# Seven-product up units of a decoder trunk: operands of VectorE moved from SBUF into PSUM banks

## The reference

```python
h2 = _modulate(_rmsnorm(x, norm_mlp_g[l]), shift2, scale2)
u = jnp.square(jax.nn.relu(h2 @ w_up[l]))        # 1024 -> 4096
x = x + gate2[:, None, :] * (u @ w_down[l])      # 4096 -> 1024
```

## Time and profile before

| | |
|---|---|
| median of three runs | 2293.23 us (2293.02 to 2293.89) |
| the profiled execution | 2292.97 us, span 2291.2 us |
| PE busy | 2259.9 us (99%) |
| DVE busy | 1295.4 us (57%) |
| ACT busy | 959.8 us (42%) |
| POOL busy | 1296.1 us (57%) |
| granted TensorE clock | 0.999 of full speed |

### The profile page before, as it was taken

How to read it: one execution, slowest core, us unless ns; L and a number is a source line. 1 busy time by engine, 2 the same in 40 slices (tenths; PEclk the granted TensorE clock), 3 DMA queues, 4 the chain that set the end, 5 groups by cost and what they waited for, 6 DMA issues and landing times.

```text
span 2291.2 us, 30815 instructions
## 1 busy us (share of the span) xinstructions
PE 2259.9 (99%) x12424; PEld 1922.8 (84%) x12424; DVE 1295.4 (57%) x1695; ACT 959.8 (42%) x1267; POOL 1296.1 (57%) x1538
## 2 busy tenths in 40 slices
PE   7999999999999999999999999999999999999999
PEld 5888888888878888898888888888888789898898
DVE  5876667546653347464576757441666534474563
ACT  4332233256675343343333323233666834343342
POOL 4454554544455458787755455454444444786883
PEclk9999999999999999999999999999999999999999
DMA  9444444422222223323334444222222222323322
GB/s 306 132 157 160 152 134 147 136 67 74 74 93 74 93 92 93 111 93 93 120 124 154 155 147 140 72 92 94 81 70 71 74 92 88 97 93 92 111 92 74
DMA packets 242094, 252.67 MB, mean 110 GB/s; under 512 B 3984, under 2 KB 237600, under 8 KB 241952
## 3 DMA queue, kind: packets, MB, share of 16 engines
q1 hardware_dynamic: 240272, 247.00, 33.4%
q10 hardware_dynamic: 1680, 3.70, 0.5%
HBM read 248.59 MB, written 2.10 MB: 109 GB/s over the span
## 4 chain that ended last, share of the span: by engine, by line
PE 89%; POOL 8%; DVE 1%; ACT 1%; DMA 0%; issue 0%; SPq 0%; DVEq 0%; ACTq 0%
PE proj L1178 54%; PE proj L1201 5%; PE proj L1235 4%; PE att L1218 4%; PE proj L1218 4%; POOL w_lo L486 4%; PE att L1501 3%; PE att L1391 2%; POOL w_lo L491 2%; POOL wx_lo L496 2%; PE att L1441 2%; PE att L1266 2%; PE proj L1266 2%; PE att L1451 1%; PE att L1429 1%; PE att L1373 1%
## 5 line engine op out<-in xcount | busy, mean ns | idle before, releaser
L516 POOL TENSOR_TENSOR w_lo<-w_raw,w_hi 128x256 fp32r<-128x256 f32 x1280 | 1038.1, 845 | 904.6 <-ACT w_hi L562 766.8
L562 ACT ACTIVATE w_hi<-w_raw 128x1024 fp32r<-128x1024 f32 (+1 forms) x300 | 303.8, 1020 | 318.3 <-PE proj L1178 189.2
L1178 PE MATMUL proj<-h_hi,w_hi 128*128 128x512 f32 x1024 | 405.5, 396 | 0.0
L1178 PE MATMUL proj<-h_hi,w_lo 128*128 128x512 f32 x1024 | 399.3, 390 | 0.0
L1178 PE MATMUL proj<-h_lo,w_hi 128*128 128x512 f32 x1024 | 398.8, 389 | 0.0
L1178 PE MATMUL proj<-y_hi,w_hi 128*128 128x512 f32 x784 | 305.2, 389 | 0.0
L1178 PE MATMUL proj<-y_lo,w_hi 128*128 128x512 f32 x784 | 305.1, 389 | 0.0
L1178 PE MATMUL proj<-y_hi,w_lo 128*128 128x512 f32 x784 | 305.0, 389 | 0.0
L1178 PEld LDWEIGHTS proj<-h_hi,w_lo 128*128 128x128 f32 x1024 | 192.1, 188 | 41.2
L1178 PEld LDWEIGHTS proj<-h_hi,w_hi 128*128 128x128 f32 x1024 | 192.4, 188 | 40.4 <-issue 1.6
L1178 PEld LDWEIGHTS proj<-h_lo,w_hi 128*128 128x128 f32 x1024 | 192.5, 188 | 37.6
(11 more groups left out here) (335 smaller groups left out, 4832.6 us busy)
## 6 DMA issues: line engine op xcount, KB each, us to landing
w_raw<-in_w_in SPq DMA_DIRECT2D x88, 1024.0 KB, 5.1
slab<-in_w_ada SPq DMA_DIRECT2D x42, 1024.0 KB, 6.3
w_raw<-in_w_up SPq DMA_DIRECT2D x32, 1024.0 KB, 5.6
w_raw<-in_w_down SPq DMA_DIRECT2D x32, 1024.0 KB, 5.1
w_raw<-in_w_ret_out SPq DMA_DIRECT2D x16, 1024.0 KB, 5.2
w_raw<-in_w_sb_out SPq DMA_DIRECT2D x8, 1024.0 KB, 5.1
w_raw<-in_w_mix_out SPq DMA_DIRECT2D x8, 1024.0 KB, 5.1
ya<-in_x SPq DMA_DIRECT2D x1, 2048.0 KB, 8.1
```

What stands on the lines that cost most here:

```text
L516: ins = pool.tensor_tensor(w_lo[:, slot, k:k + 2, :], w_raw[:, s, k:k + 2, P * j:P * (j + 1)], w_hi[:, slot, k:k + 2, :], ALU.subtract)
L562: ins = act.activation(w_hi[:, 2 * s + j, ks, :], w_raw[:, s, ks, P * j:P * (j + 1)], ACT.Copy)
L1178: last = pe.matmul(proj[:, j, :], w[:, slot, k, :], a[:, k, :], start=k == 0 and n == 0, stop=k == KT - 1 and n == 2)
```

## The change

Four buffers move from SBUF to PSUM, and two steps are written another way.

- `sums_24`, the second pair of weight sums, goes from `ya` to two whole banks: 4 and 5 of `att` for the first unit of a quarter, the two banks of `proj` for the others. `sums_31` stays in SBUF.
- The first output tile is joined in one bank, `FIRST_TILE` (bank 2): product 2 is accumulated in its left half, `joined_11` is added there in place, and `joined_12` is written to its right half. The second is joined in the chain's own bank, `joined_22` in its right half beside product 4 in its left.
- The squares `u_bank(k)` go to banks 4 and 5. ACT now takes the positive part (`Relu`, 128x512) of a joined tile to SBUF, and DVE multiplies that by the joined tile in PSUM; before, DVE squared a tile of SBUF by itself in one instruction. ACT's copy of the chain after product 4 (128x256) goes.
- The banks for products 5 and 3 and for product 2 have one copy each now in place of two, and PE's waits follow: product 5 waits for the join of the unit just before, and product 2 for its square.

The diff, cut to what the prediction speaks of:

```diff
-        sums_24 = ya[:, 6:8, :].rearrange("p a n -> p (a n)").rearrange("p (a i n) -> p a i n", a=2, i=PAIRS)
-        fifth = ada_rows
+        fifth = relu_t[:, 1, 0:HALF]
...
-        def second_bank(q):
-            return att[:, 2 + q % 2, 0:HALF]
-        def fifth_bank(q):
-            return att[:, 4 + q % 2, 0:HALF]
+        FIRST_TILE, FIFTH = att[:, 2, :], att[:, 3, 0:HALF]
+        def u_bank(k):
+            return att[:, 4 + k % 2, :]
+        def sums_24(m):
+            return (att[:, 4:6, :] if m == 0 else proj[:, :, :]).rearrange("p a (i n) -> p a i n", i=PAIRS)
...
-                def take_chain(q):
+                def relu_second(q):
                     act.wait_ge(made[4], q + 1)
-                    act.activation(relu_t[:, 1, 0:HALF], chain_bank(q), ACT.Copy).then_inc(chain_copied, 1)
+                    act.wait_ge(joined_22, q + 1)
+                    act.activation(u_t[:, 1, :], att[:, q % 2, :], ACT.Relu, scale=-1.0).then_inc(u_relued, 1)
                 def up_seven(pair, f, m):
...
                     ahead(0)
+                    if m > 0:
+                        high_u(f, 2 * m - 2)
                     act.wait_ge(made[1], q + 1)
...
                     ahead(2)
+                    if m > 0:
+                        relu_second(q - 1)
                     ahead(3)
-                    if m > 0:
-                        take_chain(q - 1)
                     ahead(4)
...
                     if m > 0:
                         high_u(f, 2 * m - 1)
-                    high_u(f, 2 * m)
+                    act.wait_ge(joined_12, q + 1)
+                    act.wait_ge(joined_11, q + 1)
+                    act.activation(u_t[:, 0, :], FIRST_TILE, ACT.Relu).then_inc(u_relued, 1)
                     if m == 3:
+                        high_u(f, 2 * m)
...
-                    if q >= 2:
-                        pe.wait_ge(joined_12, q - 1)
-                    half_product(5, wx, in_extra(s, 0), t_block(T1), fifth_bank(q), True, False)
+                    if q > 0:
+                        pe.wait_ge(joined_12, q)
+                    half_product(5, wx, in_extra(s, 0), t_block(T1), FIFTH, True, False)
...
-                    if q >= 2:
-                        pe.wait_ge(joined_11, q - 1)
-                    half_product(2, wide, in_slot(2 * s, 1), h_block(1, 0), second_bank(q), True, True)
+                    if m > 0:
+                        pe.wait_ge(u_ready, KT * (4 * layer + f) + 2 * m - 1)
+                    half_product(2, wide, in_slot(2 * s, 1), h_block(1, 0), FIRST_TILE[:, 0:HALF], True, True)
...
-                def square_u(j, bound):
-                    dve.scalar_tensor_tensor(u_t[:, j, :], relu_t[:, j, :], 0.0, relu_t[:, j, :], bound,
+                def square_first(q):
+                    dve.wait_ge(u_relued, 2 * q + 1)
+                    dve.tensor_tensor(u_bank(0), u_t[:, 0, :], FIRST_TILE, ALU.mult).then_inc(u_ready, 1)
+                def square_second(q):
+                    dve.wait_ge(u_relued, 2 * q + 2)
+                    dve.scalar_tensor_tensor(u_bank(1), u_t[:, 1, :], -1.0, att[:, q % 2, :], ALU.mult,
                                              ALU.mult).then_inc(u_ready, 1)
...
                     if m > 0:
+                        square_first(q - 1)
                         join_22(q - 1)
-                        low_u(f, 2 * m - 2)
                     if m < 3:
                         sum_weights(pair, f, m + 1)
+                    if m > 0:
+                        low_u(f, 2 * m - 2)
+                        square_second(q - 1)
+                    if m < 3:
                         low_sums(f, m + 1)
...
                     if m == 3:
+                        square_first(q)
                         join_22(q)
                         low_u(f, 2 * m)
                         square_second(q)
```

More of the change, by code:

```diff
@@ L588, in seven_split @@
                     act.wait_ge(sums_made, 3 * q + 3)
-                    ins = act.activation(wx_hi[:, s, 1:3, :, :], sums_24, ACT.Copy)
+                    ins = act.activation(wx_hi[:, s, 1:3, :, :], sums_24(m), ACT.Copy)
                 else:
@@ L1533, in up_seven @@
                     pe.wait_ge(seven_lo, 3 * q + 1)
-                    if q >= 2:
-                        pe.wait_ge(chain_copied, q - 1)
+                    if m >= 2:
+                        pe.wait_ge(u_ready, KT * (4 * layer + f) + 2 * m - 2)
                     half_product(1, wide, in_slot(2 * s, 0), h_block(0, 0), chain_bank(q), True, False)
@@ L2128, in sum_weights @@
                     dve.wait_ge(sums_made, 3 * q + 1)
-                    dve.scalar_tensor_tensor(sums_24[:, 0, :, :], block[:, A11, :, :], -1.0, sums_31[:, 1, :, :],
+                    dve.scalar_tensor_tensor(sums_24(m)[:, 0, :, :], block[:, A11, :, :], -1.0, sums_31[:, 1, :, :],
                                              ALU.mult, ALU.subtract).then_inc(sums_made, 1)
                     dve.wait_ge(sums_made, 3 * q + 2)
-                    dve.tensor_tensor(sums_24[:, 1, :, :], block[:, A12, :, :], sums_24[:, 0, :, :],
+                    dve.tensor_tensor(sums_24(m)[:, 1, :, :], block[:, A12, :, :], sums_24(m)[:, 0, :, :],
                                       ALU.subtract).then_inc(sums_made, 1)
@@ L2138, in low_sums @@
                     dve.wait_ge(seven_hi, 5 * q + 4)
-                    dve.tensor_tensor(wx_lo[:, s, 1:3, :, :], sums_24, wx_hi[:, s, 1:3, :, :],
+                    dve.tensor_tensor(wx_lo[:, s, 1:3, :, :], sums_24(m), wx_hi[:, s, 1:3, :, :],
                                       ALU.subtract).then_inc(sums_lo, 1)
@@ L2155, in join_22 @@
                     dve.wait_ge(fifth_copied, q + 1)
[L2156 to L2162, removed]
+                    dve.tensor_tensor(att[:, q % 2, HALF:SEQ], fifth, chain_bank(q), ALU.add).then_inc(joined_22, 1)
                 def up_seven(pair, f, m):
@@ L2182, in up_seven @@
                     dve.wait_ge(first_copied, q + 1)
-                    dve.tensor_tensor(relu_t[:, 0, 0:HALF], relu_t[:, 0, 0:HALF], second_bank(q),
+                    dve.tensor_tensor(FIRST_TILE[:, 0:HALF], relu_t[:, 0, 0:HALF], FIRST_TILE[:, 0:HALF],
                                       ALU.add).then_inc(joined_11, 1)
-                    dve.wait_ge(joined_12, q + 1)
-                    dve.wait_ge(joined_11, q + 1)
-                    square_u(0, ALU.max)
+                    dve.wait_ge(made[3], q + 1)
+                    dve.wait_ge(sixth_copied, q + 1)
+                    dve.tensor_tensor(FIRST_TILE[:, HALF:SEQ], relu_t[:, 0, HALF:SEQ], FIFTH,
+                                      ALU.add).then_inc(joined_12, 1)
                     if m == 3:
+                        square_first(q)
                         join_22(q)
```

18 lines of the change are left out of this document (10 added, 8 removed).

## The result

The changed kernel takes 2278.32 us (median of four runs, 2278.23 to 2278.57) against 2293.20 before (2293.02 to 2293.89): a ratio of 0.9935 with a 95% interval of 0.9918 to 0.9952, 14.9 us less. The forecast was 2277.2 us with a range of 2275.5 to 2281.5, and a chance of 0.92 for faster.

A forecast was written before the change was run, and what follows sets the result against it. PE was taken to bound the kernel, held up by POOL's late subtractions in six seven-product quarters. 2292.97 less 16.1, all else at 0, gave 2276.9 us, and 2277.2 with 0.26 for the median; range 2275.5 to 2281.5.

The forecast's parts named there:

- The bound: Six seven-product quarters: PE waits for POOL's late weight subtractions, 2.68 us a quarter, 16.1 us in all to gain.
- The cause: Up units: DVE instructions reading both inputs from SBUF lengthen POOL's subtractions from 0.74 to 1.19 or 1.72 us.
- POOL's need: POOL's ten subtractions of a unit: falls from up to 11.7 to 8.4 us, against PE's 10.1.
- DVE's and ACT's durations: Moved instructions: squares 0.69 us, joins 0.41, Relu 0.60; upper bounds 0.75 and 0.47 for squares and joins.
- The longer way of a tile: Product 2 to product 4 through joins, Relu and square: 2.47 us, hidden inside a quarter, barely in time at its end.
- The slack of 0.13: Quarter's end: join 22 done at 939.15, PE wants product 4 at 939.31; 0.13 us left after a semaphore's 0.03.
- the step of 0.065: DVE's higher fixed cost from PSUM by the Trainium skill: 0.065 us an instruction, one such step lost at the tight hand-over.
- rival A: Down unit: product 4 late at the hand-over, costing 0.2 to 0.7 us a quarter; 2278.4 to 2281.4 us, chance 0.15.
- The shares: Up units: the moved inputs were priced together, POOL's need 11.7 to 8.4 us, for one gain of 16.1 us.
- The sum: Whole kernel: 2292.97 less 16.1 gives 2276.9 us, 2277.2 with the median's 0.26; all other terms at 0.
- B: Up units: POOL stays blocked by DVE's length, output or the two remaining instructions; 2285 to 2293 us, chance 0.07.
- C: Way from product 2 to product 4 bounds a unit if its instructions take near double; 2307 us at double, chance 0.04.

The follow-up runs named there:

- e1: Changed kernel, but the six DVE instructions of a unit whose first input moved to PSUM read x_T in SBUF instead, outputs unmoved: 2295.85 us, ratio 1.0011.
- e4: Kernel before, with squares and splits of u in units 0 to 2 reading one input from a PSUM stand-in: 2277.26 us, ratio 0.9932.
- e5: Changed kernel with one more DVE square ahead of join 22 at the end of each of six quarters: 2281.67 us, ratio 0.9949.
- e2: Kernel before, with only the second pair of weight sums in PSUM, for units 1 to 3 of a quarter: 2277.46 us, ratio 0.9932.
- e8: Changed kernel with 16 waits on a long-passed semaphore added to VectorE's list: 2277.45 us.
- e9: Changed kernel with sums_24 back in SBUF and both splits of u reading x_T in SBUF: 2284.23 us, ratio 0.9961.
- e7: e2 with 108 waits on a long-passed semaphore added to ScalarE's list, 18 in each of six down stretches: 2277.32 us.

## Why the prediction was right

**The bound** (PE loses about 16 us by POOL's lateness, and that is all there is to gain): right. The starts of matmuls moved by 15.5 us, 2.58 a quarter in place of 2.68. Half of the 0.1 is the slow second start that is new at product 4 (0.04 to 0.06); the rest is rounding of the starts that I read.

**The cause** (two inputs from SBUF): right, and shown by e1 in one direction and by e4 in the other, each with the order left alone.

**POOL's need** of 8.4 us a unit: 8.35 measured in the unit shown, 8.3 in the mean. I had priced two blocks at 0.98 + 0.45 = 1.43, and they are 0.87 + 0.45 (subtractions of 1.61 and 1.19 against 0.74). The 11.7 of before was an upper bound and measures 11.1.

**DVE's and ACT's durations**: squares 0.697 against my 0.69, joins 0.422 to 0.429 against 0.41, `Relu` 0.60 against 0.60: right. The higher fixed cost of a PSUM source, which the Trainium skill gives in "VectorE: DVE Perf Modes", section on the errata of SBUF sources, isn't seen here: 0.690 for the split of u from PSUM, 0.69 for the square from SBUF before.

**The longer way of a tile**: the way itself was right. Join 22 was to end 0.16 us before product 4's start, and ends 0.17 before it (936.65 and 936.82). What follows the join was mis-sized: I gave a semaphore's 0.03 from its end to the start of product 4, and e5 shows 0.15, since the weight load comes in between (0.12 from the join's end to the load). The slack of 0.13 was 0.02. It sufficed by luck: the same sum with the right term leaves nothing for error, and the step of 0.065 that the prediction weighed and left out would have made product 4 late. A first piece of rival A is even there, the second matmul of product 4 that starts 0.05 late, 0.3 us in six quarters; it is far under A's 1.2 to 4.2.

**The shares**: here the prediction said less than it could have. It took away 3.3 of 4.7 us of lock time in a unit and asked for the sum of all of it alone; the line that it had itself drawn (11.7 against 10.1) says that 1.6 us of relief is enough. By the measured means (11.1 before, 9.2 in e2, 9.8 in e4) 1.0 is enough, and the halves take away 1.9 and 1.3. e2 has the same gain for a fraction of the edit, the place of one buffer; e4 shows it for the other half with values of u that are not the right ones.

**The sum**: 2277.2 forecast, 2278.3 measured. In the traces the span fell by 14.6 where the sum had 16.1: 0.6 is in the starts of matmuls (the bound above), and 0.9 is the last store, which was no term of the sum. That the times differ by only 1.1 comes from the 0.26 which I added for the median: it didn't come back, since the profiled execution after lies at its median. Without the late store the forecast describes e8's 2277.45. Rivals B and C didn't come true, and A only by its 0.3.

## What to carry to other kernels

When VectorE and GpSimd work beside each other, count for each unit of work GpSimd's own time plus a block for every VectorE instruction with two SBUF inputs (here 0.45 us for 512 elements and 0.87 to 0.98 for 1024), and compare it with the engine that should bound. The count is an upper bound for the mean of the units, here too high by 0.1 to 1.0 us: only the part of the relief down to that line is worth anything, so the smallest edit that crosses it will do. One input from PSUM costs VectorE nothing (0.69 us for 512 elements either way) and frees GpSimd wholly (0.73 to 0.74 us for a subtraction beside it). Where the output lies made no difference to GpSimd: e1 has outputs in PSUM and is blocked, e4 has them in SBUF and isn't. When a slack is worked out for TensorE, count from the releasing instruction's end to the matmul with its weight load in between (0.15 us here), not a semaphore alone. A microsecond that a profile can't place in the edited region may lie outside it, here at the last store: compare the distance from the last instruction of the bounding engine to the end of the span before looking for a cause in the edit.

## What the runs showed of the hardware

- An idle TensorE pays twice: in these quarters a matmul of 256 columns that starts 0.06 to 1.48 us late is followed by the next only after 0.22 us in place of 0.12, in all 18 places of the trace before, and likewise in e1 and e9. That 0.10 is 1.8 us of the 15.5. In e5, where product 4 starts 0.57 late, the next comes after 0.19.
- Which of these kernels has an 8 KB packet of the instruction queue among the packets of its last store depends on the number of records in VectorE's list, waits included. Where it lies there, one of sixteen DMA engines ends 0.8 us late and the span 0.9 us later. 16 waits more (8 records) moved it away: 5.37 in place of 6.25 us from the last matmul to the end of the span, 2277.45 against 2278.32 us in the medians. That the packet is the cause is argued and not shown.
- ScalarE is faster from PSUM: a copy of 128x512 takes 0.594 us from PSUM and took 0.632 from SBUF, one of 128x1024 1.02 against 1.06.
- e2, e4, e7 and e8 are at 2277.3 to 2277.5 us, 0.9 below the changed kernel. e2 and e8 compute all that it does; they are 0.04% faster than the changed kernel, by the last store alone. With PE no longer waiting for POOL in these quarters, nothing more is to be had there from GpSimd.
